# Router and gather of a mixture-of-experts stage: order of the crowding test, the routing weights and the constants, and the banks of the gather

## The reference

```python
logits = jnp.dot(xt, w_router).astype(jnp.float32)          # 256 tokens x 8 experts
top_logits, top_idx = lax.top_k(logits, TOP_K)              # two experts a token
top_w = jax.nn.softmax(top_logits, axis=-1).astype(u.dtype)
...
h = jax.nn.silu(lax.ragged_dot(xs, w_gate, group_sizes)) * lax.ragged_dot(xs, w_up, group_sizes)
ys = lax.ragged_dot(h, w_down, group_sizes) * top_w.reshape(-1)[order][:, None]
out = jax.ops.segment_sum(ys, tok, num_segments=n_tok)
```

## Time and profile before

| | us |
|---|---|
| median of 3 runs | 2673.63 |
| lowest and highest run | 2673.58, 2677.22 |
| span of the profiled execution, first to last instruction | 2665.3 |
| TensorE busy in it | 2537.6 |
| VectorE busy | 1703.9 |
| ScalarE busy | 1307.1 |

### The profile page before, as it was taken

The page is one execution under the profiler, slowest core; times in us unless marked ns, Lnnn a source line. Parts: engine busy times, 40 slices in busy tenths (PEclk is TensorE's granted clock), DMA queues, the critical chain, the costliest instruction groups (busy, mean ns, idle before and its releaser), DMA issues.

```text
span 2665.3 us, 32020 instructions
## 1 busy us (share of the span) xinstructions
PE 2537.6 (95%) x11890; PEld 1994.4 (75%) x11890; DVE 1703.9 (64%) x1939; ACT 1307.1 (49%) x1663; POOL 98.7 (4%) x99
## 2 busy tenths in 40 slices
PE   6998998998999999999998999989998999999996
PEld 3656884656888888888876888878876887897884
DVE  2566445558999999999986544555555543455555
ACT  2333432326877877878863442444433443443441
POOL 1020001020000000000001000000000000000001
PEclk9999997999999999999999999999999999999998
DMA  8846548736999999999994553345534553326541
GB/s 344 283 166 197 189 159 326 274 106 241 392 366 353 363 358 351 368 348 362 362 318 149 187 202 99 111 154 189 189 111 164 200 176 136 117 96 217 189 173 48
DMA packets 316099, 608.64 MB, mean 228 GB/s; under 512 B 14706, under 2 KB 154002, under 8 KB 309315
## 3 DMA queue, kind: packets, MB, share of 16 engines
q1 hardware_dynamic: 309312, 583.14, 61.5%
q0 software_dynamic: 6384, 22.75, 2.4%
q10 hardware_dynamic: 274, 1.05, 0.1%
HBM read 605.83 MB, written 1.05 MB: 228 GB/s over the span
## 4 chain that ended last, share of the span: by engine, by line
PE 85%; DVE 8%; DMA 3%; ACT 2%; issue 1%; POOL 1%; SPq 0%; DVEq 0%; ACTq 0%
PE G L864 49%; PE A L864 29%; PE TB L864 4%; DMA down<-in_ada_w 1%; PE TB L886 1%; DVE w_lo L2492 1%; POOL small L2308 1%; PE TB L1171 1%; DVE small L2784 1%; DVE u_lo L2736 1%; DMA wide<-in_ffn_w_in 1%; PE TB L1254 1%; DMA down<-in_moe_w_down 1%; DVE x_tok L2773 1%; DVE x_tok L2796 1%
## 5 line engine op out<-in xcount | busy, mean ns | idle before, releaser
L864 PE MATMUL G<-w_hi,u_hi 128*128 128x512 f32 x1584 | 629.6, 397 | 12.0 <-DVE u_lo L2736 7.1
L864 PE MATMUL G<-w_lo,u_hi 128*128 128x512 f32 x1584 | 620.1, 391 | 0.0
L864 PE MATMUL G<-w_hi,u_lo 128*128 128x512 f32 x1584 | 619.7, 391 | 0.0
L2511 DVE TENSOR_TENSOR w_lo<-wide,w_hi 128x1024 fp32r<-128x1024 f32 x352 | 415.2, 1220 | 14.2 <-ACT w_hi L1928 4.1
L1928 ACT ACTIVATE w_hi<-wide 128x1024 fp32r<-128x1024 f32 x352 | 370.9, 1062 | 91.5 <-PE G L864 44.2
L864 PEld LDWEIGHTS G<-w_hi,u_hi 128*128 128x128 f32 x1584 | 299.0, 189 | 77.0 <-DVE w_lo L2492 12.1
L864 PEld LDWEIGHTS G<-w_hi,u_lo 128*128 128x128 f32 x1584 | 299.0, 189 | 64.6
L864 PEld LDWEIGHTS G<-w_lo,u_hi 128*128 128x128 f32 x1584 | 299.2, 189 | 59.8 <-issue 0.2
L864 PE MATMUL A<-w_hi,hidden_hi 128*128 128x512 f32 x792 | 309.6, 391 | 0.0
L864 PE MATMUL A<-w_hi,hidden_lo 128*128 128x512 f32 x792 | 308.5, 390 | 0.0
L864 PE MATMUL A<-w_lo,hidden_hi 128*128 128x512 f32 x792 | 308.2, 389 | 0.0
(11 more groups left out here) (344 smaller groups left out, 3286.0 us busy)
## 6 DMA issues: line engine op xcount, KB each, us to landing
down<-in_moe_w_down SPq DMA_DIRECT2D x176, 512.0 KB, 8.2
wide<-in_ffn_w_in SPq DMA_DIRECT2D x88, 1024.0 KB, 7.6
wide<-in_moe_w_gate SPq DMA_DIRECT2D x160, 512.0 KB, 8.0
wide<-in_moe_w_up SPq DMA_DIRECT2D x160, 512.0 KB, 8.8
down<-in_ffn_w_out SPq DMA_DIRECT2D x44, 1024.0 KB, 8.6
down<-in_ada_w SPq DMA_DIRECT2D x40, 1024.0 KB, 6.8
wide<-in_w_in SPq DMA_DIRECT2D x24, 1024.0 KB, 8.0
wide<-in_fox_w_in SPq DMA_DIRECT2D x12, 1024.0 KB, 5.5
```

The costliest lines, as they stand in the source:

```text
L864: return nc.tensor.matmul(o, lhsT, rhs, start=start, stop=stop, skip_group_check=True)
L2511: V.tensor_tensor(w_lo[at % RING][:, :], raw_piece(n, at)[0], w_hi[at % RING][:, :].bitcast(F32), ALU.subtract).then_inc(lo_ready, 1)
```

## The change

- In `router`, VectorE makes `slotid` and `crowded` directly behind `source_low(0)`. The softmax and routing weights move into `route_weights`, which in the packed branch runs behind the low part of piece 3, and in the other branch first. The second `source_low` runs behind `pick`.
- TensorE's `keep_clock(6)` between the branch and the gather is gone; `keep_clock(2)` stands before the ranks and another behind them.
- The gather of the first pair of experts uses banks 0 and 1 of A for even groups and 2 and 3 for odd ones, so that group j waits for the copies of group j - 2. Its first low product waits for the second `source_low`.
- VectorE's order in the first pair is: `pick`, `source_low(1)`, `rest` 0, copies 0 and 1, `rest` 1, copies 2 and 3, `rest` 2 and 3, `route_weights`, then on from piece 4.
- The slot weights of the first pair are made by TensorE behind the first unit's gates, into bank 1 of TB.

```diff
+        def gather_bank(j):
+
+            return 2 * (j % 2)
...
                     if p:
                         pe.wait_ge(moe_silu, p * 2 * UNITS - 1)
+                    else:
+                        pe.wait_ge(moe_routed, 1)
+                    bank = G[:, 0, :] if p else TB[:, 1, :]
...
-                        if p or j:
-                            pe.wait_ge(evacuated, 4 * p + j)
+                        if p or j >= 2:
+                            pe.wait_ge(evacuated, 4 * p + (j if p else j - 1))
+                        if p == 0 and j == 0 and at:
+                            pe.wait_ge(moe_src_lo, T)
+                        bank = at if p else gather_bank(j) + at
...
-                    if j == 0:
+                    if j == 0 and p:
                         slot_weights(p)
...
-                pe.wait_ge(acc_free, n.free)
-                keep_clock(6, A[:, 3, :])
                 pe.wait_ge(moe_src_hi, T)
-                pe.wait_ge(moe_src_lo, T)
...
                             gates(p, e, u)
+                            if (p, e, u) == (0, 0, 0):
+                                slot_weights(0)
...
+                    pe.wait_ge(acc_free, n.free)
+                    keep_clock(2, A[:, 3, :])
                     pe.wait_ge(dve_ready, n.dve + 2)
                     for t in range(T):
...
                         last.then_inc(g_done, 1)
+                    keep_clock(2, A[:, 3, :])
...
+            def route_weights(n):
+
+                scratch = rsum[:, :, 0:EXPERTS]
+                dve.wait_ge(act_ready, n.act + 1)
+                link(V.tensor_scalar(w1, e2, 1.0, None, ALU.add))
+                link(V.reciprocal(w1, w1))
+                link(V.tensor_tensor(w2, e2, w1, ALU.mult))
+                for t in range(T):
+                    V.tensor_scalar(scratch[:, t, :], C("experts"), idxf[:, t, 0:1], w1[:, t:t + 1], ALU.is_equal, ALU.mult)
+                    link(V.tensor_scalar(route[:, t, :], C("experts"), idxf[:, t, 1:2], w2[:, t:t + 1],
+                                         ALU.is_equal, ALU.mult))
+                for t in range(T):
+                    last = V.tensor_tensor(route[:, t, :], route[:, t, :], scratch[:, t, :], ALU.add)
+                last.then_inc(moe_routed, 1)
+                dve.wait_ge(moe_routed, 1)
...
                 picks(0)
-                for q in range(2):
-                    rest(0, q)
-                for j in range(4):
-                    gathered(0, j)
-                    if j == 0:
-                        slot_weights(0)
+                source_low(1)
+                rest(0, 0)
+                gathered(0, 0)
+                gathered(0, 1)
+                rest(0, 1)
+                gathered(0, 2)
+                gathered(0, 3)
+                for at in (2, 3):
+                    rest(0, at)
+                route_weights(steps[MOE_AT - 1][2])
...
                         rest(p, at)
+                        if p == 0 and at == RING - 1:
+                            slot_weights(0)
...
                     source_low(0)
-                    dve.wait_ge(act_ready, n.act + 1)
-                    link(V.tensor_scalar(w1, e2, 1.0, None, ALU.add))
-                    link(V.reciprocal(w1, w1))
-                    link(V.tensor_tensor(w2, e2, w1, ALU.mult))
-                    source_low(1)
                     dve.wait_ge(dve_ready, n.dve + 2)
-                    for t in range(T):
-                        link(V.tensor_scalar(rtmp[:, t, :], C("experts"), idxf[:, t, 0:1], w1[:, t:t + 1],
-                                             ALU.is_equal, ALU.mult))
-                        link(V.tensor_scalar(route[:, t, :], C("experts"), idxf[:, t, 1:2], w2[:, t:t + 1],
-                                             ALU.is_equal, ALU.mult))
-                        link(V.tensor_tensor(route[:, t, :], route[:, t, :], rtmp[:, t, :], ALU.add))
```

## The result

| | before | after |
|---|---|---|
| median, first comparison | 2673.61 us (4 runs) | 2657.14 us (4 runs) |
| ratio, 95% interval | | 0.9941, 0.9929 to 0.9954 |
| ratio, second and third comparison | | 0.9951 (0.9937 to 0.9964), 0.9957 (0.9945 to 0.9970) |
| span of the profiled execution | 2665.3 us | 2649.6 us |

I forecast 2664.0 us in a range of 2661.5 to 2668.5 and measured 2657.14. The direction was right, the range missed on the far side. In the two repeats the changed kernel's medians were 2658.74 and 2660.25.

The account below looks back on a forecast made before the run. TensorE bounds the kernel, transfers close behind; 21.7 us lie between the experts' marks and the first expert product. An earlier start gains 10.9 us, less 0.95 and 0.3, so 9.6: 2673.6 becomes 2664.0 us, range 2661.5 to 2668.5.

Parts of the forecast that it names:

- The test behind the ranks: In the router, slot numbers and crowding test no longer wait behind unrelated VectorE work: gain 3.33 us.
- The constants hidden in the waits: Router: clock-keeping passes before and behind the ranks fit TensorE's waits; cost taken as 0, bound 1.4 us.
- The long fill gone: Between branch and gather: without twelve constant passes TensorE meets `pick` itself; 6.7 us of the 10.9 gained.
- VectorE as the bound of the start: Gather: VectorE's row of 7.04 us from `pick` sets the experts' start, S, taken as 613.5 against 624.41.
- Slot weights coming back between gates and ups: First expert unit: eight single-column products leave the gather but cost 0.95 us between gates and ups.
- Routing weights covered behind piece 3: First expert unit: about 1.85 us of VectorE routing work stays hidden behind TensorE; cost 0, bound 1.1 us.
- rival 2: First expert units: VectorE and transfers both lag and TensorE stalls; gain 7.2 us, time 2665.8 us; chance 0.13.
- Rival 3: Expert stage is bound by transfers, so some 8 us are returned: 2672 us, no measurable change; chance 0.11.
- Rival 4: Clock stays low into the experts' dense products; slower from 20 us of them, 32 us gives 2680; chance 0.03.
- The median lies 8.3 us above that span and I carry it over unchanged: Final sum: 8.3 us between before's profiled span, 2665.3, and its median, 2673.6, kept when forecasting the new median.
- rival 1: Clock falls in the gather: gain 6.1 us if low throughout, some 8.5 if regained midway; middle 2666.3; chance 0.26.
- The clock rule that spoke against the change: Gather: a matmul stream cycling through banks pauses enough for the clock to fall, so it would run at 1.2 GHz.

Follow-up runs that it names:

- r11: Kernel before with only slot numbers and crowding test moved directly behind the ranks; executed once, first expert product 18.1 us after the experts' marks, 21.7 in before.
- r3: Changed kernel without its two keep_clock(2) in the router; ratio to before 0.9969 (0.9955 to 0.9982).
- r6: Changed kernel with the routing weights put back ahead of the slot numbers; executed once, first expert product 14.2 us after the experts' marks, 10.3 in the changed kernel.
- r2: Changed kernel again, no edit; median 2658.74 us, ratio to before 0.9951 (0.9937 to 0.9964).
- r10: Changed kernel a third time, no edit; median 2660.25 us, ratio to before 0.9957 (0.9945 to 0.9970).
- r7: Changed kernel with one pair of banks for the gather; executed once, first expert product 12.0 us after the experts' marks, 10.3 in the changed kernel.
- r5: Kernel before with only keep_clock(6) taken out; executed once, first expert product 17.7 us after the experts' marks, 21.7 in before.
- r12: Changed kernel without the constants ahead of the ranks, those behind kept; executed once, first expert product 11.2 us after the experts' marks, 10.3 in the changed kernel.
- r1: Kernel before again, no edit; ratio to before 0.9998 (0.9989 to 1.0007).
- r9: Kernel before a third time, no edit; ratio to before 0.9998 (0.9989 to 1.0007).

## Why the prediction was right and where it failed

*What held.* The test behind the ranks: 3.33 us forecast; 5.6 to 2.2 us after the marks is 3.4, r11 gave 3.6 alone. The constants hidden in the waits: yes, and r3 shows in one trace what they hold. The long fill gone: yes. VectorE as the bound of the start: S at 10.3 us after the marks where the sum gave 10.8 (613.5 - 602.7) and the signs 10.4 to 11.2; the groups stood 0.48 us apart, shorter than my shortest, and the second half of the source cost 1.15 as counted. The trace of before had that distance, in the gather of the second pair. There TensorE came from dense products without a fill, so the prediction's remark that no gather runs without the fill is wrong; but this one says nothing of a gather behind an idle stretch:

```profile
803.33 0.64 PE L864 MATMUL A<-pick,l_hi 128*128 128x256 f32 x4
803.80 0.64 PE L864 MATMUL A<-pick,l_lo 128*128 128x256 f32 x4
```

Slot weights coming back between gates and ups: 0.79 us against 0.95. Routing weights covered behind piece 3: the chain of after runs from product to product there. Backlog (rival 2): none. Of TensorE's matmuls after's waits from 611 to 700 (engine line waited for: us in total, times, longest) have one row, the wait ahead of the first product:

```profile
PE G L871 <- issue: 1.2, 1, 1.2
```

Rival 3, start without effect at the end: no, 9.2 of the 11.4 us arrive at the end of the section. 1.0 on average is the router's own matmuls at low clock in two of three traces of after. The other 1.2 lie behind the first product. 0.4 of them are in the experts' products up to ScalarE's `packed_hi` (from the first product to it 771.1, 770.5 and 772.2 us in before, 771.2, 771.9 and 771.9 in after). 0.8 are in the stretch from there to the section's end (13.4, 13.5, 14.0 against 14.0, 14.8, 14.5), where the last eight products took 2.9 to 3.8 us in all three of after at a fallen clock, and in two of three traces of before only four of them, 1.17 us, stand in the chain (rows of before, then of after):

```profile
1398.05 1.17 PE A L864 x4
```

```profile
1385.40 2.88 PE A L871 x8
```

Rival 4 did not occur: from the first product to the section's end the clock is 0.99 to 1.00 in all six traces.

So the forecast of 9.6 us was right for the section, 9.2 us measured in three traces each, and its mechanism held. That the two are so near is in part luck. Start and products gained 11.0 us (11.4 less 0.4), more than the 9.95 of the sum, and 1.8 more than in before went to a low clock, in the router and behind the last products, for which the sum had no term. In the nine traces of the changed kernel and its variants the router met the low clock three times, in those of after two times in three. So the three of after may have had more than their share, which would be some of the 3 us; that is not shown.

*The step that failed* is "The median lies 8.3 us above that span and I carry it over unchanged", and with it the range. The 8.3 us are not a fixed part around the span. Every timed execution of the two kernels stands about 1.8 us above its own span (2651.34 over 2649.6). The other 6.5 us are the distance from an execution that happened to be short to a median of three that was high: 68 executions of the kernel before have spans from 2664.5 to 2675.3 us, with a mean of 2669.2, or 2671.0 in time. The forecast lies 6.9 us above the measured 2657.14, in three parts. 2.6 us are the base, a median of 2673.6 for a kernel whose mean is 2671.0; from there 9.6 us lead to 2661.4, not 2664.0. 2.4 us are the gain, 12.0 in the mean of the timed executions where I had 9.6; the traced section gave 9.2, so this part stays open. 1.9 us are chance on the other side: the fourteen executions of the changed kernel have a mean time of 2659.0, and the four of the first comparison a median of 2657.14. My range took in every unknown cost of the change and nothing for the medians of three or four runs, which move by 2 us and more each. The first comparison, at 16.5 us between medians, was also at the far side; the two repeats gave 11.0 and 10.7.

*A size within the section* was wrong in its reading, not its sum: I priced rival 1, a gather at half clock, at 2.3 us over the forecast in the middle. r3 measured 1.2: the low groups stood closer than I had counted, only five of eight were low, and VectorE, which sets the end, took up 0.4. In r6, where seven of the eight were low, the clock added 1.9.

The clock rule that spoke against the change (the Trainium skill, TensorE: Matmul & The Clock Gate, section A second HAM failure mode: psum-queue depth-cycling), by which a stream that cycles through PSUM banks pauses often enough for the clock to swing, did not come true for the gather itself: with two pairs of banks it ran at 1.00 in after, r2 and r10, and with one pair, in r7, too. Where the clock was low in the gather or the fill (before, r3, r5, r6, r11 and r12), a wait of 2.0 us or more stood ahead of the fall or around it. The wait alone doesn't decide: six traces came through the one ahead of the ranks at 1.00, and r12 didn't.

## What to carry to other kernels

- A filler that keeps the clock belongs into the waits, where it costs nothing; in front of ready work it costs whatever of its length that work could have used, here 3.6 of 5.4 us for twelve passes at high clock.
- On a path with a clock that falls in idle time, price an operation twice: once for its length and once for the idle time that it makes on TensorE. In the one trace of r6, 1.9 us of small operations cost 3.8.
- Before carrying a profile's sum to a median, subtract the profiled execution's own span from typical spans. If one trace is several us below the median, that distance is scatter and belongs into the range, not into the sum.

## What the runs showed of the hardware that I had not expected

The granted clock fell at quite different idle times. It fell in r12 in a wait of 2.1 us ahead of the ranks, 1.2 us into it. Behind the end of the ranks it fell after 0.4 to 0.9 us in before, r1, r9, r3, r5 and r11, and in r6 2.7 us behind the end of the constants. In after, r7 and r10 it fell in the router's matmuls, behind the transposes of the second tile, with no gap over 1.6 us just ahead of them; in the other eleven traces the same matmuls ran at 1.00. In after, r2, r7 and r10 a gap of 1.2 us ahead of the gather left it at 1.00. In before it came back after 5.5 us of dense passes, in r6 after 6.4 us of the light gather. The same code in the same kernel meets either clock, and the router's 24 matmuls then take 3.0 or 4.5 us.
